# Weights and activations multiplied as plain float32, one product a tile, in place of three products of split float32r parts

## The chip, the cores and the metric

The kernel runs on one core of a Trainium2 chip. The metric is the device time of one launch in microseconds (us). Three runs of the kernel before gave 3092.03 us in the median (3088.94 to 3093.2).

## The reference

Two transformer stacks run one after the other on one sequence of 256 tokens by 1024 channels, all in float32. Cut to its products:

```python
# first stack, two layers: mixer, then FFN (layer 0 dense, layer 1 eight experts, top 2)
for layer in range(2):
    x = x + hybrid_mixer(rms_norm(x), w_in[layer], ...)   # 1024 x 9216, then three 1024 x 1024
    x = x + swiglu(h, w1, w3, w2)                         # layer 0: 1024 x 2816 twice, 2816 x 1024
    x = x + moe_swiglu(h, router_w, w1, w3, w2)           # layer 1: the same for each of 8 experts
x = rms_norm(x, final_norm)
# second stack, four layers: hyena, window attention, pooling, hyena; each with a swiglu
for i in range(4):
    x = x + mixer_i(rmsnorm(x))
    x = x + (silu(xn @ wg) * (xn @ wu)) @ wd
```

Nearly all arithmetic is activations times weights. The rest (chunked recurrence, convolutions by DFT, attention scores, routing, norms) works on tiles of the 256 tokens.

## The kernel before

Every weight matrix is cut into panels of 1 MB (128 partitions by 2048 floats; the last panel of each column block of an FFN's down projection has 1536). `panel_list` gives their order, and `sp_panels` (L236) loads them in that order from SyncE's queue into the `raw` ring of 6 places, each once panel i - 6 is `used`. A panel is 8 k-tiles of 256 columns in most products, so 16 weight tiles of 128x128, each met by the 256 tokens. For the experts it is 4 k-tiles of 512 columns (or 8 of 256), and in the expert's down projection 2 k-tiles of 1024; there the activations of 128 gathered tokens stand still in the array and the weights stream past.

TensorE gets float32r operands in two parts. ScalarE writes the rounded part of a panel into `whi`, a ring of 4 (`act_feed`, L251 to L260), and VectorE writes the rest, raw minus `whi`, over the raw panel as `wlo` (`dve_feed`, L263 to L271). `act_panel` and `dve_panel` put these instructions, up to three panels ahead, between the other work of the two engines; each engine works strictly in its order. Activations are kept in two parts as well: `act_high` or `act_ahead` on ScalarE, then `dve_low` (L470) or `dve_ahead` (L430) on VectorE. A tile's product is then three matmuls:

```python
e.matmul(o, wh, xh, start=first and t == k0, stop=False)   # L327
e.matmul(o, wh, xl, start=False, stop=False)               # L328
i = e.matmul(o, wl, xh, ...)                               # L329
```

L566 to L568, L1142 to L1144 (expert down), L1163 to L1165 (expert up and gate), L1997 to L1999 and L2233 to L2235 do the same for other shapes. `pe_panel` waits for both parts of the panel.

Other products were plain float32 before and stay so: the sums of squares (L354), the scores of the recurrence (L628), the DFTs (L1612, L1642, L1657), the scatter of expert outputs (L1212) and the transposes. The program text has one matmul for each such product.

Each stage is written by hand for each engine. In `pe_hgrn` the mixer's columns come in the order f, q, v, then ten half-steps with the recurrence's scores between them, gb, then `conv` on `CX`, `proj` on `OX`, `out` on `HX`. The last chunk of `CX` follows from `dve_conv` (L832), that of `HX` for `out` from L814, L816, `act_high` and L470. `pe_ffn` runs 11 pairs of panels and 12 down panels. `pe_moe` gathers tokens for a pair of experts (L1194), runs both experts and scatters (L1212).

Of the kernel before, what the change touches and what calls it, by code (L numbers as in the profile page):

```python
# [8 lines left out]
F32R = mybir.dt.float32r  # L9
# [7 lines left out]
L = 256  # L17
T8 = 8
# [4 lines left out]
NRAW = 6  # L23
NSPLIT = 4
# [14 lines left out]
def columns():  # L39
# [15 lines left out]
    "raw0", "raw1", "raw2", "raw3", "raw4", "raw5",  # L55
    "x_in", "ident_in", "vectors_in", "consts_in", "misc_in", "bias_in", "sink_in", "feat_in", "hy_in",
# [5 lines left out]
class Book:  # L62
# [6 lines left out]
    def restart(self, counting=False):  # L69
        self.counting = counting  # L70
        self.count = dict.fromkeys(self.sem, 0)
        self.turn, self.held, self.owner = 0, set(), [None] * 8
        self.panels = dict.fromkeys(("pe", "act", "dve"), 0)
        self.fed = dict.fromkeys(("act", "dve"), 0)
# [53 lines left out]
class Memory:  # L128
    def __init__(self, nc, ctx):
# [4 lines left out]
        self.HX = sb("HX", [128, 2, T8, L], F32R)  # L134
        self.HXP = nc.alloc_sbuf_tensor_at("HXP", [128, 2 * BUF], F32, offset=nc.sbuf_base - 8 * BUF)
        self.raw = sb("raw", [128, NRAW, BUF])
        self.wlo = nc.alloc_sbuf_tensor_at("wlo", [128, NRAW, BUF], F32R, offset=nc.sbuf_base - 4 * NRAW * BUF)
        self.whi = sb("whi", [128, NSPLIT, BUF], F32R)
# [11 lines left out]
        base = nc.sbuf_base - 4 * WORK  # L150

        def rounded(name, i, shape):
            return nc.alloc_sbuf_tensor_at(name, shape, F32R, offset=base + int(4 * BUF * i))

        self.OX = rounded("OX", 8, [128, 2, T8, L])
        self.CX = rounded("CX", 5, [128, 7, T8, L])[:, 0:7:6]
        self.HID = rounded("HID", 0, [128, 2, 22, L])
        self.HT = [rounded("HTH", 0, [128, 22, 128]), rounded("HTL", 1.5, [128, 22, 128])]
        self.GT = [rounded("GT0", 3, [128, 8, 2, L]), rounded("GT1", 5, [128, 8, 2, L])]
        self.SELR = rounded("SELR", 8, [128, 2, 2, 128])  # L160
        self.HXB = rounded("HXB", 6, [128, 2, T8, L])
# [23 lines left out]
def panel_list(a):  # L185
# [26 lines left out]
    hgrn(0)  # L212
    ffn(a["dense_w1"][0], a["dense_w3"][0], a["dense_w2"][0])
# [37 lines left out]
def act_feed(e, k, m, panels):  # L251
    i = k.fed["act"]
    if i == len(panels):
        return
    k.fed["act"] += 1
    n = width(panels[i])
    e.wait_ge(*k.at("raw", i))
    if i >= NSPLIT:
        e.wait_ge(*k.at("used", i - NSPLIT))
    e.activation(m.whi[:, i % NSPLIT, 0:n], m.raw[:, i % NRAW, 0:n], ACT.Copy).then_inc(*k.up("act", "hi", i))  # L260


def dve_feed(e, k, m, panels):  # L263
    i = k.fed["dve"]
    if i == len(panels):
        return
    k.fed["dve"] += 1
    n = width(panels[i])
    e.wait_ge(*k.at("hi", i))
    hi = m.whi[:, i % NSPLIT, 0:n].bitcast(F32)  # L270
    e.tensor_tensor(m.wlo[:, i % NRAW, 0:n], m.raw[:, i % NRAW, 0:n], hi, ALU.subtract).then_inc(*k.up("dve", "lo", i))  # L271


def act_panel(e, k, m, panels):

    k.panels["act"] += 1
    while k.fed["act"] < min(k.panels["act"] + NSPLIT - 1, 2 * k.panels["act"] + 1, len(panels)):
        act_feed(e, k, m, panels)


def dve_panel(e, k, m, panels):
    k.panels["dve"] += 1
    while k.fed["dve"] < min(k.panels["dve"] + NSPLIT - 1, 2 * k.panels["dve"] + 1, len(panels)):
        dve_feed(e, k, m, panels)


def pe_panel(e, k, m):
    i = k.panels["pe"]
    k.panels["pe"] += 1
    e.wait_ge(*k.at("hi", i))  # L290
    e.wait_ge(*k.at("lo", i))
    return i


def weights(m, i, kt, n):
    both = m.whi[:, i % NSPLIT, 0:kt * n], m.wlo[:, i % NRAW, 0:kt * n]
    return [w.rearrange("p (k n) -> p k n", k=kt) for w in both]
# [21 lines left out]
def pe_weights_still(e, k, o, w, c, x, k0, k1, kx, first=True, final=True, fresh=None):  # L319

    i = None
    for t in range(k0, k1):
        wh, wl = (v[:, t, c:c + 128] for v in w)
        xh, xl = x[:, 0, kx + t, :], x[:, 1, kx + t, :]
        if fresh:
            e.wait_ge(*k.at(*fresh, kx + t))
        e.matmul(o, wh, xh, start=first and t == k0, stop=False)  # L327
        e.matmul(o, wh, xl, start=False, stop=False)  # L328
        i = e.matmul(o, wl, xh, start=False, stop=final and t == k1 - 1)  # L329
    return i  # L330


def pe_gemm(e, k, m, s, name, x, cols, fresh=None, after=None):

    for j in cols:
        i = pe_panel(e, k, m)
        w = weights(m, i, 8, 256)
        o = pe_take(e, k, m, "g", s, name, j)
        pe_weights_still(e, k, o[:, 0:L], w, 0, x, 0, 8, 0, fresh=fresh)
        fresh = None  # L340
        pe_weights_still(e, k, o[:, L:2 * L], w, 128, x, 0, 8, 0).then_inc(*k.up("mm", "g", s, name, j))
# [37 lines left out]
def act_norm(e, k, m, s, h, rstd):  # L379
    act_rstd(e, k, m, s, rstd)  # L380
    for c in range(T8):
        e.wait_ge(*k.at("h", s, c))
        e.activation(m.HX[:, 0, c, :], h[:, c, :], ACT.Copy).then_inc(*k.up("act", "hh", s, c))


def dve_scale(e, k, m, s, c, h, rstd, gain):
# [11 lines left out]
def dve_norm(e, k, m, s, h, rstd, gain):  # L398
    for c in range(T8 + 1):
        if c < T8:  # L400
            dve_scale(e, k, m, s, c, h, rstd, gain)
# [2216 lines left out]
```

## Time and profile before

| | |
|---|---|
| median of 3 runs | 3092.03 us |
| the profiled execution, device time | 3087.74 us |
| its span in the profile | 3085.9 us |
| TensorE matmul busy | 2980.6 us (97%) |
| VectorE busy | 2039.1 us (66%) |
| ScalarE busy | 1632.0 us (53%) |
| granted TensorE clock, mean | 0.98 of full |
| read from HBM | 608.99 MB |

Busy time of TensorE counts pipelined matmuls once. The duration of one record (0.28 us for one of 256 columns) is its latency, longer than the distance to the next record's start. What a stream of matmuls costs is read from the starts. The chain of waits lists each step with that distance.

### The profile page before, as it was taken

What the parts mean: (1) busy time and instruction counts of PE and PEld (TensorE: products, weight loads), DVE (VectorE), ACT (ScalarE), POOL (GpSimd) and SP (SyncE); (2) the same over time, 40 slices, a digit from 0 to 9 for tenths busy, and PEclk for the clock granted to TensorE, in tenths of its full rate; (3) what the DMA queues carried; (4) which work ended last, traced back from release to release, by engine and by line L of the source; (5) the groups of instructions that cost most, each with busy time, mean ns of one, the idle gap of its engine ahead of it and who ended that gap; (6) DMA issues with size and microseconds to landing.
All of it is one profiled execution on the core that took longest, in us unless ns stands there. A gap on an engine that the chain in (4) does not pass through costs nothing.

```text
span 3085.9 us, 46925 instructions
## 1 busy us (share of the span) xinstructions
PE 2980.6 (97%) x20370; PEld 2732.1 (89%) x20370; DVE 2039.1 (66%) x1833; ACT 1632.0 (53%) x1593; POOL 260.0 (8%) x199
## 2 busy tenths in 40 slices
PE   7999999999979999999999899999899999999999
PEld 7998999999878888888788596999799999886999
DVE  5786665578648888888789665554555455565553
ACT  5446444544537767777677452444654444363442
POOL 1130110013000000000000102010001001012010
PEclk9999999999979999999999899999999999999999
DMA  6444555544428989989989240556255555431453
GB/s 206 156 139 144 157 178 177 179 151 144 144 98 347 356 341 375 350 339 358 367 341 371 93 137 28 166 183 213 82 160 178 195 164 172 157 107 58 137 179 122
DMA packets 358818, 613.14 MB, mean 199 GB/s; under 512 B 11375, under 2 KB 323397, under 8 KB 323536
## 3 DMA queue, kind: packets, MB, share of 16 engines
q1 hardware_dynamic: 354592, 597.73, 55.5%
q10 hardware_dynamic: 3536, 12.23, 1.2%
q8 instruction: 164, 2.69, 0.4%
q14 instruction: 46, 0.38, 0.0%
q0 software_dynamic: 480, 0.12, 0.0%
HBM read 608.99 MB, written 1.05 MB: 198 GB/s over the span
## 4 chain that ended last, share of the span: by engine, by line
PE 86%; DVE 5%; ACT 5%; issue 2%; DMA 1%; ACTq 0%; DVEq 0%
PE ps L327 16%; PE ps L328 16%; PE ps L329 16%; PE ps L1163 5%; PE ps L1165 5%; PE ps L1164 5%; PE ps L1144 3%; PE ps L1142 3%; PE ps L1143 2%; PE ps L1642 2%; PE ps L628 2%; PE ps L1657 2%; ACT whi L260 2%; PE ps L1612 1%; DVE wlo L271 1%
## 5 line engine op out<-in xcount | busy, mean ns | idle before, releaser
L271 DVE TENSOR_TENSOR wlo<-raw,whi 128x2048 fp32r<-128x2048 f32 (+1 forms) x573 | 1315.4, 2301 | 633.6 <-ACT whi L260 629.5
L260 ACT ACTIVATE whi<-raw 128x2048 fp32r<-128x2048 f32 (+1 forms) x573 | 1083.7, 1894 | 271.1 <-PE ps L329 139.6
L327 PE MATMUL ps<-HX,whi 128*128 128x256 f32 x1808 | 520.5, 288 | 26.2 <-DVE HX L470 10.7
L328 PE MATMUL ps<-HX,whi 128*128 128x256 f32 x1808 | 514.8, 285 | 0.0
L329 PE MATMUL ps<-HX,wlo 128*128 128x256 f32 x1808 | 514.8, 285 | 0.0
L327 PE MATMUL ps<-HXB,whi 128*128 128x256 f32 x1760 | 500.3, 284 | 0.0
L329 PE MATMUL ps<-HXB,wlo 128*128 128x256 f32 x1760 | 498.1, 283 | 0.0
L328 PE MATMUL ps<-HXB,whi 128*128 128x256 f32 x1760 | 498.0, 283 | 0.0
L327 PEld LDWEIGHTS ps<-HX,whi 128*128 128x128 f32 x1808 | 350.4, 194 | 29.6 <-DVE HX L470 16.3
L328 PEld LDWEIGHTS ps<-HX,whi 128*128 128x128 f32 x1808 | 350.4, 194 | 0.6 <-issue 0.2
L329 PEld LDWEIGHTS ps<-HX,wlo 128*128 128x128 f32 x1808 | 350.2, 194 | 0.0
L327 PEld LDWEIGHTS ps<-HXB,whi 128*128 128x128 f32 x1760 | 337.9, 192 | 0.7 <-issue 0.3
L328 PEld LDWEIGHTS ps<-HXB,whi 128*128 128x128 f32 x1760 | 337.8, 192 | 0.3
L329 PEld LDWEIGHTS ps<-HXB,wlo 128*128 128x128 f32 x1760 | 337.8, 192 | 0.0
L1163 PE MATMUL ps<-whi,GT 128*128 128x512 f32 (+1 forms) x768 | 289.4, 377 | 4.7 <-DVE wlo L271 4.3
L1165 PE MATMUL ps<-whi,GT 128*128 128x512 f32 (+1 forms) x768 | 286.3, 373 | 0.0
L1164 PE MATMUL ps<-wlo,GT 128*128 128x512 f32 (+1 forms) x768 | 285.8, 372 | 0.0
L327 PE MATMUL ps<-HID,whi 128*128 128x256 f32 x880 | 251.2, 285 | 0.0
L329 PE MATMUL ps<-HID,wlo 128*128 128x256 f32 x880 | 249.1, 283 | 0.0
L328 PE MATMUL ps<-HID,whi 128*128 128x256 f32 x880 | 249.0, 283 | 0.0
L1163 PEld LDWEIGHTS ps<-whi,GT 128*128 128x128 f32 x768 | 145.1, 189 | 29.9 <-DVE wlo L271 3.8
L327 PEld LDWEIGHTS ps<-HID,whi 128*128 128x128 f32 x880 | 168.9, 192 | 0.3
(318 smaller groups left out, 4382.6 us busy)
## 6 DMA issues: line engine op xcount, KB each, us to landing
raw<-in_c_experts SPq DMA_DIRECT2D x264, 1024.0 KB, 4.9
raw<-in_w_in SPq DMA_DIRECT2D x72, 1024.0 KB, 5.0
raw<-in_ff_w_gate SPq DMA_DIRECT2D x44, 1024.0 KB, 5.3
raw<-in_ff_w_up SPq DMA_DIRECT2D x44, 1024.0 KB, 5.3
raw<-in_ff_w_down SPq DMA_DIRECT2D x32, 1024.0 KB, 5.1
raw<-in_dense_w SPq DMA_DIRECT2D x30, 1024.0 KB, 5.3
raw<-in_hy_w_in SPq DMA_DIRECT2D x24, 1024.0 KB, 5.2
raw<-in_ff_w_down SPq DMA_DIRECT2D x16, 768.0 KB, 4.5
```

What stands on the lines that cost most here:

```text
L260: e.activation(m.whi[:, i % NSPLIT, 0:n], m.raw[:, i % NRAW, 0:n], ACT.Copy).then_inc(*k.up("act", "hi", i))
L271: e.tensor_tensor(m.wlo[:, i % NRAW, 0:n], m.raw[:, i % NRAW, 0:n], hi, ALU.subtract).then_inc(*k.up("dve", "lo", i))
L327: e.matmul(o, wh, xh, start=first and t == k0, stop=False)
L328: e.matmul(o, wh, xl, start=False, stop=False)
L329: i = e.matmul(o, wl, xh, start=False, stop=final and t == k1 - 1)
L628: mm = e.matmul(o[:, c * 128:(c + 1) * 128], lhs[:, hh], rhs[:, hh], start=True, stop=True)
L1142: e.matmul(o[c][:, :], hh, wh[:, kk, cs], start=t == 0, stop=False)
L1143: e.matmul(o[c][:, :], hh, wl[:, kk, cs], start=False, stop=False)
L1144: mm = e.matmul(o[c][:, :], hl, wh[:, kk, cs], start=False, stop=t == 21)
L1163: e.matmul(o[:, 0:n], xh, wh[:, t, :], start=first, stop=False)
L1164: e.matmul(o[:, 0:n], xh, wl[:, t, :], start=False, stop=False)
L1165: mm = e.matmul(o[:, 0:n], xl, wh[:, t, :], start=False, stop=last)
```

## The change

The split goes. Panels are multiplied from the place where they land, in float32, with activations kept once, in float32. The `raw` ring has 10 places, in the room of `whi` and the second half of the activations. Both engines' feeds go (L251 to L284), as do all high and low parts. The gather of the experts' tokens makes one float32 product where it made two float32r ones. Smaller edits come with it:

- the first panel of the program comes in two halves, x as well, and the six DMAs of constants that ScalarE issued are issued by SyncE behind the first ten panels; the sums of squares of x come after the first gemm in place of before it (`pe_first`)
- activations for the next gemm are scaled by ScalarE for even chunks and by VectorE for odd ones (`act_ahead`, `dve_ahead`)
- the first tap of the mixer's convolution is a ScalarE instruction (`taps`), and chunks 4 to 7 are convolved before the norm of gb in place of behind it
- the four norms of o come together behind the first conv panel, and the output leaves in four DMAs

```diff
-NRAW = 6
-NSPLIT = 4
+NRAW = 10
-def act_feed(e, k, m, panels):
-    e.activation(m.whi[:, i % NSPLIT, 0:n], m.raw[:, i % NRAW, 0:n], ACT.Copy).then_inc(*k.up("act", "hi", i))
-def dve_feed(e, k, m, panels):
-    e.tensor_tensor(m.wlo[:, i % NRAW, 0:n], m.raw[:, i % NRAW, 0:n], hi, ALU.subtract).then_inc(*k.up("dve", "lo", i))
+def pe_panel(e, k, m, kt, n):
+    i = k.panels
+    k.panels += 1
     e.wait_ge(*k.at("raw", i))
+    return i, m.raw[:, i % NRAW, 0:kt * n].rearrange("p (k n) -> p k n", k=kt)
...
-        e.matmul(o, wh, xh, start=first and t == k0, stop=False)
-        e.matmul(o, wh, xl, start=False, stop=False)
-        i = e.matmul(o, wl, xh, start=False, stop=final and t == k1 - 1)
+        i = e.matmul(o, w[:, t, c:c + 128], x[:, kx + t, :], start=first and t == k0, stop=final and t == k1 - 1)
...
+def pe_first(e, k, m, s, last):
+    for h in range(2):
+        i, w = pe_panel(e, k, m, 4, 256)
+        halves.append(w)
+        pe_weights(e, k, o[:, 0:L], w, 0, m.HX, 0, 4, 4 * h, first=h == 0, final=h == 1, fresh=("hx", last))
+    for h in range(2):
+        mm = pe_weights(e, k, o[:, L:2 * L], halves[h], 128, m.HX, 0, 4, 4 * h, first=h == 0, final=h == 1)
...
-                    e.matmul(o[c][:, :], hh, wh[:, kk, cs], start=t == 0, stop=False)
-                    e.matmul(o[c][:, :], hh, wl[:, kk, cs], start=False, stop=False)
-                    mm = e.matmul(o[c][:, :], hl, wh[:, kk, cs], start=False, stop=t == 21)
+                    mm = e.matmul(o[c][:, :], m.HT[:, t, :], w[:, kk, c * 512:c * 512 + 512], start=t == 0, stop=t == 21)
...
+    def taps(cs):
+        e.wait_ge(*k.at("free", "g", s, "u", 3))
+        for c in cs:
+            e.activation(m.buf8(5)[:, c, :], conv_rows(m)[:, c, 0:L], ACT.Copy, scale=m.col("conv_w", 24 * l + c)).then_inc(
+                *k.up("act", "tap", s, c))
...
     for j in range(4):
-        dve_panel(e, k, m, panels)
+        dve_conv(e, k, m, s, l, (4 + j,))
         dve_times_norm(e, k, m, s, last, "gb", j, m.buf(1)[:, j * 512:j * 512 + 512])
-        dve_conv(e, k, m, s, l, (4 + j,))
...
-    e.dma_start(out, m.X[:, :, :]).then_inc(*k.land("out_done", "out"))
+    for c0, c1 in ((0, 4), (4, 6), (6, 7), (7, 8)):
+        for c in range(c0, c1):
+            e.wait_ge(*k.at("x", last, c))
+        e.dma_start(out[:, c0:c1, :], m.X[:, c0:c1, :]).then_inc(*k.land("out_done", "out"))
```

TensorE's queue from the start of the program before (`HX` is the activations, `ones` serves the sums of squares):

```order
L354 MATMUL ps<-work,ones 128x256 x6
L327 MATMUL ps<-HX,whi 128x256
L328 MATMUL ps<-HX,whi 128x256
L329 MATMUL ps<-HX,wlo 128x256
L327 MATMUL ps<-HX,whi 128x256
```

The same queue now (`rows` is the activations, `raw` the panels as landed):

```order
L275 MATMUL ps<-rows,raw 128x256 x16
L307 MATMUL ps<-work,ones 128x256 x8
L275 MATMUL ps<-rows,raw 128x256 x112
L381 MATMUL ps<-ident,rs 128x128 x2
L283 MATMUL ps<-raw,rows 128x256 x64
```

The 48 matmuls of a panel are 16, and the sums of squares stand behind the first of them.

VectorE's queue before, from the last chunk of the mixer's convolution through the conv products to the start of `proj`'s:

```order
L842 SCALAR_TENSOR_TENSOR work<-work,par 128x256
L845 TENSOR_TENSOR work<-work 128x256
L470 TENSOR_TENSOR CX<-work,CX 128x256
L271 TENSOR_TENSOR wlo<-raw,whi 128x2048
L808 TENSOR_TENSOR work<-work,ps 128x512
L796 SCALAR_TENSOR_TENSOR work<-work,par 128x512
L800 TENSOR_TENSOR work<-work 128x512
L796 SCALAR_TENSOR_TENSOR work<-work,par 128x512
L800 TENSOR_TENSOR work<-work 128x512
L470 TENSOR_TENSOR OX<-work,OX 128x256 x4
L271 TENSOR_TENSOR wlo<-raw,whi 128x2048
```

And now (L366 is the norm of the last gb panel):

```order
L755 SCALAR_TENSOR_TENSOR work<-work,par 128x256
L757 SCALAR_TENSOR_TENSOR work<-work,par 128x256
L760 TENSOR_TENSOR work<-work 128x256
L366 TENSOR_TENSOR work<-ps,rs 128x512
L729 TENSOR_TENSOR work<-work,ps 128x512
L719 SCALAR_TENSOR_TENSOR work<-work,par 128x512
L723 TENSOR_TENSOR work<-work 128x512
L719 SCALAR_TENSOR_TENSOR work<-work,par 128x512
L723 TENSOR_TENSOR work<-work 128x512
```

The last chunk of the convolution is complete before the last gb panel is normed, and neither a low part nor a panel's split stands between.

## Rows read from the trace of the kernel before

**Rows 1.** The page: busy time by engine; granted TensorE clock in 40 slices.

```profile
PE 2980.6 (97%) x20370; PEld 2732.1 (89%) x20370; DVE 2039.1 (66%) x1833; ACT 1632.0 (53%) x1593; POOL 260.0 (8%) x199
...
PEclk9999999999979999999999899999999999999999
```

**Rows 2.** The page: costliest groups, the two feeds.

```profile
L271 DVE TENSOR_TENSOR wlo<-raw,whi 128x2048 fp32r<-128x2048 f32 (+1 forms) x573 | 1315.4, 2301 | 633.6 <-ACT whi L260 629.5
L260 ACT ACTIVATE whi<-raw 128x2048 fp32r<-128x2048 f32 (+1 forms) x573 | 1083.7, 1894 | 271.1 <-PE ps L329 139.6
```

**Rows 3.** Chain of waits, last FFN: start us, us to the next, what.

```profile
3068.12 0.12 PE ps L327
...
3071.72 0.12 PE ps L327
```

**Rows 4.** Chain of waits, an expert's down projection.

```profile
999.93 0.23 PE ps L1144
...
1001.97 0.23 PE ps L1144
```

**Rows 5.** Timeline of PE, plain float32 streams: start us, us, what, records.

```profile
1138.57 7.07 PE L1212 MATMUL ps<-work 128*128 128x256 f32 x32
...
1877.90 13.98 PE L1657 MATMUL ps<-work 128*128 128x256 f32 x64
...
1759.57 8.32 PE L1612 MATMUL ps<-work 128*128 128x512 f32 x19
```

**Rows 6.** PE groups by line and shape: xcount | busy us, mean ns | idle before.

```profile
L327 PE MATMUL ps<-HX,whi 128*128 128x256 f32 x1808 | 520.5, 288 | 26.2 <-DVE HX L470 10.7 <-DVE wlo L271 6.3 <-issue 4.9
...
L327 PE MATMUL ps<-HXB,whi 128*128 128x256 f32 x1760 | 500.3, 284 | 0.0
...
L1163 PE MATMUL ps<-whi,GT 128*128 128x512 f32 x640 | 252.6, 395 | 4.7 <-DVE wlo L271 4.3 <-ACT GT L1280 0.3
L327 PE MATMUL ps<-HID,whi 128*128 128x256 f32 x880 | 251.2, 285 | 0.0
...
L1142 PE MATMUL ps<-whi,HTH 128*128 128x512 f32 x352 | 138.5, 394 | 0.0
...
L327 PE MATMUL ps<-CX,whi 128*128 128x256 f32 x128 | 39.7, 310 | 11.8 <-DVE CX L470 11.8
```

**Rows 7.** Whom PE waited for: us in total, times, longest us.

```profile
PE ps L327 <- DVE CX L470: 11.8, 2, 5.9
...
PE ps L327 <- DVE HX L470: 10.7, 3, 5.2
...
PE ps L1938 <- ACT small L2067: 5.2, 2, 2.7
PE ps L327 <- issue: 4.9, 2, 3.6
...
PE ps L1163 <- DVE wlo L271: 4.3, 2, 3.4
PE ps L327 <- ACT HX L466: 4.2, 2, 2.1
```

**Rows 8.** Timeline of the start, PE.

```profile
9.46 4.53 PE L354 MATMUL ps<-work,ones 128*128 128x256 f32 x12 [9.46 <-ACT work L361]
20.33 0.55 PE L327 MATMUL ps<-HX,whi 128*128 128x256 f32 x1 [6.34 <-DVE wlo L271]
```

**Rows 9.** Windows behind three waits, PE: us, PE busy (records), PEclk, DMA share, GB/s.

```profile
275.70:282.60 6.90, 2.97 (x14) 0.51 0.00 1
...
866.20:873.10 6.90, 5.67 (x26) 0.51 0.00 0
1531.80:1535.30 3.50, 3.50 (x10) 0.51 1.02 424
```

**Rows 10.** Window over the experts: us, PE, PEld, DVE, ACT, POOL, PEclk, DMA, GB/s.

```profile
926.20:1717.60 791.40, 785.05 (x3772) 660.12 (x3772) 671.05 (x399) 572.12 (x405) 0.00 (x0) 1.00 0.92 353
```

**Rows 11.** Timeline of the end, the output's DMA, in a span of 3085.9.

```profile
3081.63 0.36 SPq L2336 DMA_DIRECT2D out<-X  x1
```

## What the change will do: the prediction

> **What bounds the kernel now.** I read the page's busy times first: TensorE is busy for 2980.6 of 3085.9 us, VectorE for two thirds and ScalarE for half [rows 1]. The two feeds look expensive, 1315.4 us of VectorE and 1083.7 us of ScalarE [rows 2], but both engines wait for TensorE or for each other most of the time, so they count only where TensorE waits for them. I therefore read next whom TensorE waited for [rows 7], and last how far apart its matmuls start, from the chain of waits [rows 3, 4] and the timeline [rows 5]. The reader is to see that TensorE is idle for 3085.9 - 2980.6 = 105 us in all, and that the change's sign depends on one comparison: three float32r matmuls against one plain float32 product.
>
> **A tile of 256 columns before.** From 3068.12 to 3071.72 the chain has 30 steps [rows 3], 3.60 / 30 = 0.120 us each, so three make 0.360 us.
>
> **A tile of 512 columns before.** From 999.93 to 1001.97 there are 9 steps [rows 4], 0.227 us each, so three make 0.680 us.
>
> **A plain float32 product.** The text has 16 matmuls for one scatter (4 x 2 x 2 in `pe_scatter`), yet the timeline has 32 records for it [rows 5]; the start shows 12 records for 6 matmuls of L354 [rows 8]. Every plain product is thus two records, and each record takes long. L1657 has 64 records of 256 columns in 13.98 us; less the latency of the last one (0.38), that is 13.60 / 63 = 0.216 us each. L1212 gives the same: (7.07 - 0.38) / 31 = 0.216. One product of 256 columns is 0.432 us. L1612 has 19 records of 512 columns in 8.32 us: (8.32 - 0.59) / 18 = 0.429, so a product is 0.859 us. The weights change with every product in L1657 and L1612, both operands come from SBUF, and the clock is full, as it will be here. float32r pays its 0.120 with a change of weights each time as well.
>
> So a tile of 256 columns gets slower by 0.432 - 0.360 = 0.072 us, one of 512 by 0.859 - 0.680 = 0.179 us.
>
> A page of the Trainium skill bears on this. "FP8 and Floating Point Precision", TensorE Precision Notes, says that true FP32 takes four passes through the array; "TensorE: Matmul & The Clock Gate", Back-to-back issue gap, gives a warm pass N / 2.4 + 2.5 ns. Four such passes are 0.437 and 0.863 us, an estimate from the pages. The rows say 0.432 and 0.859, so here two of the four passes share one record and its fixed cost. The same formula gives a float32r pass of 256 columns 0.109 us, and the row's 0.120 disagrees; the row decides. By the pages' cost of the new products alone the sum below would be 28 us higher.
>
> **How many tiles.** The first of the three matmuls is counted by shape [rows 6]: 1808 (HX) + 1760 (HXB) + 880 (HID) + 128 (CX), three more groups of 128 that the text gives (OX, the experts' last columns, the v columns) and two of 16 (attention's v, pooling) make 4992 of 256 columns; 640 + 352 = 992 have 512. 4992 x 0.072 = 359 us, and 992 x 0.179 = 178 us. The gather of a pair of experts goes from 32 float32r matmuls (3.84 us) to 16 plain ones (6.9 us), four times: 12 us. Together +549 us. The text's other products stay.
>
> **What comes back.**
> - The start. The first gemm begins at 20.33 us, 6.34 us after the early sums and waiting for `wlo` [rows 8]. Now half of x, half a panel and one scaling suffice. I take 8 to 9 us, since ScalarE's first work on x ended before the sums began at 9.46. Of these 12 us, 2.6 go to the six sums that used to run in the idle time, and about 1.3 to more tiles at the half clock. Gain 8 us.
> - The waits of the mixers. CX 11.8, HX 10.7, two "issue" waits 4.9 (one of them behind VectorE's scan, where a split stood queued), the experts' `wlo` 4.3, the hyena's HX 4.2 [rows 7]: 35.9 us. In each the last chunk now needs one or two instructions where it needed four, and `out` has six tiles of 0.43 us to run before it wants that chunk. What is late next is the last evacuation of `proj`, two VectorE instructions of 512 columns, which I estimate from the duration of a 2048-column one [rows 2] at under 2 us with their waits, against 2.6. I take all 35.9.
> - Attention's waits for ScalarE, 5.2 [rows 7], where feeds stood between squares. I take 5.
> - The clock. Behind each of these waits the granted clock fell from 1.0 to 0.5, 1.2 GHz of 2.4: at 275.7, 866.2 and 1531.8 [rows 9], and three times more. A stretch holds 14 to 26 matmuls of 0.213 us in place of 0.120 (about 2 us), the expert's 10 lose 0.2 each. Six together 11 us.
> - The end. The output's DMA starts at 3081.63 and ends the span at 3085.9 [rows 11], 4.3 us for 1 MB. The last of four pieces is an eighth: 2 us less.
>
> That is 8 + 36 + 5 + 11 + 2 = 62 us. VectorE loses 1315 us and ScalarE 1084 us of feeds and gain nothing by it otherwise; the taps, copies and scalings that move to ScalarE are below 1 us each and lie beside gemms. The ring of ten panels gains nothing either: over the experts the DMA engines moved 353 GB/s [rows 10] in 791 us; now the same bytes have some 980 us, 285 GB/s. The waits that I leave (routing, the branch before the second stack, hyena's transposes, some 45 us) depend on chains that the change barely shortens.
>
> **The sum.** The profiled execution took 3087.7 us: 3087.7 + 549 - 62 = 3575. It lies 4.3 us below the median of the three runs, so the time forecast for the median is 3579 us, 16% slower. The bounds: none of the waits behind the start returned gives 3087.7 + 549 - 10 + 4 = 3631; all of TensorE's idle time and some 25 us of half clock returned gives 3087.7 + 549 - 130 + 4 = 3511.
>
> **The rivals.**
> 1. Much more comes back (3511 us). For it: VectorE and ScalarE are half empty afterwards, and every handover has fewer steps. Against: routing and the second stack's start wait for chains without a feed in them. 8%.
> 2. Little comes back (3631 us). The waits named move to what is late next, the POOL's norms or ScalarE's longer chain at `on`, and the half clock with them. For it: all four `on` products now stand behind the first conv panel and read squares that ScalarE makes from the o products. Against: a panel now takes 6.9 us where it took 5.8, so each such chain has more cover. 13%.
> 3. The new products cost the pages' four full passes, or weights that come from a place beside a landing DMA cost a little more: 3607 us. 6%.
> 4. Faster: each new product is one record of 0.216 (0.429) us. The mechanism would be that the second record belongs to something particular to the old plain products. Then the tiles change by 4992 x -0.144 + 992 x -0.251 = -968 us, less 62; the experts would be bound by DMA, 264 panels or 277 MB at the 353 GB/s of [rows 10] being 785 us against 511 us of matmuls, which gives 274 back: about 2330 us. The change is a gain as soon as a 256-column product costs under about 0.37 us. Against it: three lines of different operands all show two records per product. 2%.
> 5. The clock stays at 0.5 in these streams, over 6000 us. L1612 and L1657 ran at the full clock through tens of us. 1%.
>
> **How the numbers follow.** My forecast, between about 3545 and 3615, has 70%. With part of rivals 1 to 3 the range of 3535 to 3622 holds the time 8 times in 10. A change under 0.2% (6 us) couldn't be told from none. Faster 2% (rival 4), the same 1%, slower 97%.
>
> **What would show it.** In the changed profile the L275 matmuls have two records for each in the text (about 9,984 of 256 columns), with starts 0.216 us apart; expert records are 0.429 apart; TensorE is over 97% busy; the first gemm begins at 8 to 9 us; no wait stands before the conv or out gemm of either mixer; the slices over the experts move some 285 GB/s. I am wrong if records of 256 columns start less than 0.18 us apart or come one to a product, if the idle time of TensorE exceeds 80 us, or if the clock falls in the middle of a gemm.

## The result, and the profile after

The changed kernel took 3563.56 us in the median of 4 runs (3561.89 to 3567.58), the kernel before 3092.61 us in the runs beside it: a ratio of 1.1527, with a 95% interval of 1.1508 to 1.1547, so it is 15% slower. The forecast was 3579 us, 15 us more. Profile against profile the execution took 3562.73 us where before took 3087.74: +475.0 us, and the forecast was +487.

The page of the changed kernel, busy times and clock, answers to [rows 1]:

```profile
PE 3506.4 (98%) x14386; PEld 2643.8 (74%) x14386; DVE 625.7 (18%) x1019; ACT 502.4 (14%) x850; POOL 213.5 (6%) x199
...
PEclk9999999999989999999999899999999999999999
```

TensorE has 14386 records in place of 20370 and is busy 526 us longer. VectorE lost 1413 us and ScalarE 1130 us, and nothing was won by it. The groups of matmuls by line and shape of the changed kernel (count, busy time, latency of one, idle time before) answer to [rows 6]:

```profile
L275 PE MATMUL ps<-work,raw 128*128 128x256 f32 x5792 | 1254.9, 379 | 0.0
L275 PE MATMUL ps<-rows,raw 128*128 128x256 f32 x3616 | 790.5, 380 | 8.9 <-DMA raw<-in_w_in 8.9
L1052 PE MATMUL ps<-raw,work 128*128 128x512 f32 x1280 | 554.7, 592 | 0.3 <-ACT work L1163 0.3
L1035 PE MATMUL ps<-raw,work 128*128 128x512 f32 x704 | 304.8, 592 | 0.0
L283 PE MATMUL ps<-raw,rows 128*128 128x256 f32 x320 | 69.7, 379 | 0.0
...
L1052 PE MATMUL ps<-raw,work 128*128 128x256 f32 x256 | 56.6, 379 | 0.0
```

5792 + 3616 + 320 + 256 = 9984 records of 256 columns are two for each of 4992 tiles, and 1280 + 704 = 1984 are two for each of 992. The pace stands in the changed kernel's chain of waits (start, us to the next, what, records), which answers to [rows 3, 4]:

```profile
252.37 41.44 PE ps L275 x192
...
2263.12 170.94 PE ps L275 x792
```

170.94 / 792 = 0.216 us for a record of 256 columns. In an expert's up and gate products (L1052) 10 records of 512 columns take 4.29 us, 0.429 each:

```profile
1179.96 4.29 PE ps L1052 x10
```

Whom TensorE waited for in the changed kernel (us in total, times, longest) answers to [rows 7]:

```profile
PE ps L275 <- DMA raw<-in_w_in: 8.9, 1, 8.9
PE ps L1460 <- issue: 5.8, 1, 5.8
PE ps L1493 <- DVE work L1701: 5.4, 2, 2.7
PE ps L992 <- DVE work L335: 3.9, 1, 3.9
PE ps L1004 <- DVE work L1206: 3.7, 1, 3.7
PE ps L1780 <- ACT small L1900: 3.1, 2, 1.5
```

No wait for the activations of `conv` or `out` is left. What is left are the first panel's landing, the second stack's beginning (L1460), the hyenas, the routing (L992, L1004) and attention. All of TensorE's idle time is 3560.9 - 3506.4 = 54.5 us, where it was 105.3. The changed kernel's timeline of the start and of the end answers to [rows 8, 11]:

```profile
8.88 9.15 PE L275 MATMUL ps<-rows,raw 128*128 128x256 f32 x32 [8.88 <-DMA raw<-in_w_in]
17.87 3.62 PE L307 MATMUL ps<-work,ones 128*128 128x256 f32 x16
...
3555.99 2.92 SPq L2140 DMA_DIRECT2D out<-X  x2
3558.13 0.42 DVE L886 TENSOR_TENSOR X<-X,ps 128x256 f32<-128x256 f32 x1 [2.17 <-PE ps L275]
```

The first gemm starts at 8.88 us, 11.5 us sooner. The span ends at 3560.9, 2.4 us after VectorE's last addition; before, it ended 4.4 us after that addition. A window over the experts of the changed kernel (us, PE, PEld, DVE, ACT, POOL, granted clock, DMA share, GB/s) answers to [rows 10]:

```profile
1030.00:2005.00 975.00, 973.82 (x2644) 484.42 (x2643) 46.23 (x86) 72.50 (x129) 0.00 (x0) 1.00 0.81 287
```

The DMA engines moved 287 GB/s in place of 353, with a share of 0.81 in place of 0.92, and TensorE was busy for 973.8 of the 975 us.

### The profile page after: what moved, and what is told of

The parts are those of the page before. It is cut to its first block, busy times and chain, and to the rows that moved or that the text cites. A ratio compares the mean times of both kernels' runs of the same rounds, so it can differ in the third digit from the quotient of the medians.

```text
span 3560.9 us, 32658 instructions
## 1 busy us (share of the span) xinstructions
PE 3506.4 (98%) x14386; PEld 2643.8 (74%) x14386; DVE 625.7 (18%) x1019; ACT 502.4 (14%) x850; POOL 213.5 (6%) x199
## 4 chain that ended last, share of the span: by engine, by line
PE 97%; ACT 1%; DVE 1%; issue 0%; POOL 0%; DMA 0%; ACTq 0%; SPq 0%; POOLq 0%; DVEq 0%
PE ps L275 57%; PE ps L1052 17%; PE ps L1035 8%; PE ps L283 2%; PE ps L1504 2%; PE ps L568 2%; PE ps L1519 2%; PE ps L1474 1%; PE ps L307 1%; PE ps L1083 1%; PE ps L1460 1%; PE ps L1101 1%; PE ps L1069 1%; PE ps L1814 0%; PE ps L2056 0%
## 5 line engine op out<-in xcount | busy, mean ns | idle before, releaser
L275 PE MATMUL ps<-work,raw 128*128 128x256 f32 x5792 | 1254.9, 379 | 0.0
L275 PEld LDWEIGHTS ps<-work,raw 128*128 128x128 f32 x5792 | 1100.2, 190 | 150.7 <-issue 1.3
L275 PE MATMUL ps<-rows,raw 128*128 128x256 f32 x3616 | 790.5, 380 | 8.9 <-DMA raw<-in_w_in 8.9
L275 PEld LDWEIGHTS ps<-rows,raw 128*128 128x128 f32 x3616 | 686.6, 190 | 102.8 <-DMA raw<-in_w_in 8.9
L1052 PE MATMUL ps<-raw,work 128*128 128x512 f32 (+1 forms) x1536 | 611.3, 557 | 0.3 <-ACT work L1163 0.3
L1052 PEld LDWEIGHTS ps<-raw,work 128*128 128x128 f32 x1536 | 289.5, 190 | 301.0 <-issue 294.2
L1035 PE MATMUL ps<-raw,work 128*128 128x512 f32 x704 | 304.8, 592 | 0.0
L1035 PEld LDWEIGHTS ps<-raw,work 128*128 128x128 f32 x704 | 132.5, 190 | 160.7 <-issue 160.7
L366 DVE TENSOR_TENSOR work<-ps,rs 128x512 f32<-128x512 f32 x84 | 58.0, 691 | 775.5 <-issue 526.5
L864 POOL TENSOR_TENSOR work<-work,rs 128x512 f32<-128x512 f32 x55 | 69.7, 1268 | 1092.1 <-ACT work L853 1092.1
L372 POOL TENSOR_TENSOR work<-work,rs 128x512 f32<-128x512 f32 x40 | 51.2, 1280 | 371.4 <-ACT work L575 370.7
L283 PE MATMUL ps<-raw,rows 128*128 128x256 f32 x320 | 69.7, 379 | 0.0
L1474 PE MATMUL ps<-work 128*128 128x512 f32 x128 | 60.6, 635 | 3.1 <-issue 3.1
L1504 PE MATMUL ps<-work 128*128 128x512 f32 x128 | 58.2, 612 | 3.1 <-ACT work L1569 3.0
```

The lines of the kernel that those rows point to most:

```text
L275: i = e.matmul(o, w[:, t, c:c + 128], x[:, kx + t, :], start=first and t == k0, stop=final and t == k1 - 1)
L283: i = e.matmul(o[:, j * 256:j * 256 + 256], x[:, t, j * 128:j * 128 + 128], w[:, t, :], start=t == t0, stop=t == t1 - 1)
L366: e.tensor_tensor(dst.rearrange("p (a n) -> p a n", a=2), o, m.wide_rs, ALU.mult).then_inc(*k.up("dve", "free", "g", s, name, j))
L372: e.tensor_tensor(v, v, m.wide_rs, ALU.mult).then_inc(*k.up("pool", *event))
L864: e.tensor_tensor(v, v, m.wide_rs, ALU.mult).then_inc(*k.up("pool", "sil normed", s, j))
L1035: mm = e.matmul(o[c][:, :], m.HT[:, t, :], w[:, kk, c * 512:c * 512 + 512], start=t == 0, stop=t == 21)
```

## Where the 475 us come from

From the matmul records of both traces I worked out an account of the span: for each pair of neighbours, the distance of their starts less the median distance of that line and shape at the full clock. What is over 0.4 us counts as a wait; what is less counts as half clock where the granted clock was 0.5.

| | before | after | difference | forecast |
|---|---|---|---|---|
| records at their full-clock pace | 2924.5 | 3472.1 | +547.6 | +549 |
| waits between records | 111.6 | 59.9 | -51.7 | -49 |
| half clock | 26.5 | 10.5 | -16.0 | -11 |
| the rest of short gaps | 8.7 | 6.3 | -2.4 | 0 |
| before the first and behind the last record | | | about -2.5 | -2 |

The sum is +475. (These waits begin at the median distance and not at the end of a record's latency, so they add up to more than the page's idle time.) The new products cost what the rows of the old plain ones said. The waits came back nearly as forecast in size. This doesn't say which part of the change gave them back. The experiments are about that.

## Experiments on the changed kernel

Each expectation says what its own theory A and theory B are. In the first, theory A is the prediction's: the handovers to TensorE have fewer steps, so their waits go. Theory B: the steps don't matter; a panel now takes 6.9 us of TensorE in place of 5.8, and this covers the same chains.

**plain_in_old.** The kernel before, feeds, low parts and waits all kept, with one plain matmul a tile (here at L327; the five other sites alike). The low parts enter no product, so this kernel leaves them out of its result:

```diff
-        e.matmul(o, wh, xh, start=first and t == k0, stop=False)
-        e.matmul(o, wh, xl, start=False, stop=False)
-        i = e.matmul(o, wl, xh, start=False, stop=final and t == k1 - 1)
+        i = e.matmul(o, wh.bitcast(F32), xh.bitcast(F32), start=first and t == k0, stop=final and t == k1 - 1)
```

> The kernel before with one thing changed: each weight tile is met by one plain float32 product of the two high parts, in place of three float32r products. Both engines still make every high and low part, and TensorE still waits for both; the low parts enter no product, so that part of the result is left out. Theory A (the price of the product makes the slowdown, and the rest of the change gave back some 75 us): 4992 x 0.072 + 992 x 0.175 = 533 us on top of 3092, less what the longer gemms hide by themselves, so 3600 to 3625 us. Theory B (the feeds' removal gives back nothing, the longer gemms hide the old waits by themselves): within 10 us of the changed kernel less its 12 us of dearer gathers, so 3545 to 3560 us.

3569.45 us, ratio 1.1546 (1.1527 to 1.1565). Both ranges missed it, and B was nearer, by 9 us against 31. The time is 6 us above the changed kernel's, 18 if one adds the 12 us by which its gathers are cheaper. What is left of waits behind a feed or a handover of `HX`:

```profile
PE ps L327 <- DVE wlo L271: 5.4, 1, 5.4
...
PE ps L327 <- ACT HX L464: 4.2, 2, 2.1
```

The 11.8 us for CX and the 10.7 us for HX [rows 7] are gone although no step of the handovers was taken away. So a longer panel is enough to remove them, and the prediction's reason isn't needed for it. The account of the span, worked out for this run as well, says where it differs from the changed kernel: about 12 us less for the gathers, and against that 12 us more of waits, 4 of half clock and 3 before the first and behind the last record.

**ring6, old_start, old_mixer_order.** In each of these, one group of the smaller edits of the changed kernel is undone: `NRAW = 6` in place of 10; the first panel whole and the sums of squares before the first gemm; the taps on VectorE, conv behind gb's norm and the norms of o in two pairs.

```diff
-NRAW = 10
+NRAW = 6
```

```diff
-    for c0 in (0, 4):
-        e.dma_start(m.X[:, c0:c0 + 4, :], a["c_x"][:, c0:c0 + 4, :]).then_inc(*k.land(f"x{c0 // 4}_in"))
...
+    e.dma_start(m.X[:, :, :], a["c_x"]).then_inc(*k.land("x0_in"))
```

```diff
-        w1, w2 = (m.col("conv_w", (l * 3 + j) * 8 + c) for j in (1, 2))
-        e.wait_ge(*k.at("tap", s, c))
+        w0, w1, w2 = (m.col("conv_w", (l * 3 + j) * 8 + c) for j in range(3))
...
+        e.tensor_scalar(o, vp[:, c, 0:L], w0, None, ALU.mult).then_inc(*k.up("dve"))
```

> The changed kernel with 6 panel places in place of 10. Theory A (DMA is late nowhere): no change, 3560 to 3570 us. Rival (the deeper ring is what removed the two waits over the experts, 4.3 us and the half clock behind them): 3568 to 3575 us, with waits of PE for DMA of raw.

> The changed kernel with the start of before: x and the first panel whole, the constants' DMAs on ScalarE's queue ahead of its work, the sums of six chunks before the first gemm. Theory A: the first gemm begins some 4 to 5 us later (at 13 to 14 us in place of 8.9), but 2.6 us of sums move into the idle time, so 1 to 3 us slower. Rival (the start edits carry the whole gain of 8 us at the start): 3571 us.

> The changed kernel with the mixer's old order in both layers: the first tap on VectorE, chunks 4 to 7 convolved behind the norm of gb, the norms of o in two pairs. Theory A (the waits of 11.8 us for CX went because the split's instructions went): no wait comes back, 3560 to 3567 us. Rival (they went by the new order): 10 to 18 us slower, 3574 to 3582 us, with PE waiting for VectorE's last chunk before the conv gemm.

They took 3564.32, 3563.09 and 3562.75 us against 3563.56: undone one at a time, none of the three moves the time beyond its spread from run to run. With old_start the first gemm began at 14.06 us in place of 8.88, but by then twelve records of the sums of squares were done, and its 32 records took 7.07 us, 0.216 each. In the changed kernel the 32 took 9.15 us: its first ten start about 0.43 us apart, twice the distance of the rest, and those slow records are here among the sums of squares, of which the first ten cost as much. The rows of old_start:

```profile
14.06 7.07 PE L273 MATMUL ps<-rows,raw 128*128 128x256 f32 x32
20.96 1.03 PE L305 MATMUL ps<-work,ones 128*128 128x256 f32 x4
```

The same 48 records are done by 21.83 us here and by 21.32 in the changed kernel.

## The loop that TensorE waited for

A longer panel can only cover a wait if what TensorE waits for has a period of its own. The kernel before's timeline of VectorE over the gb panels of the first mixer, its feeds only:

```profile
253.20 2.29 DVE L271 TENSOR_TENSOR wlo<-raw,whi 128x2048 fp32r<-128x2048 f32 x1 [1.38 <-ACT whi L260]
...
260.14 2.29 DVE L271 TENSOR_TENSOR wlo<-raw,whi 128x2048 fp32r<-128x2048 f32 x1 [1.38 <-ACT whi L260]
...
267.08 2.29 DVE L271 TENSOR_TENSOR wlo<-raw,whi 128x2048 fp32r<-128x2048 f32 x1 [1.37 <-ACT whi L260]
```

and of ScalarE in the same place:

```profile
258.21 1.90 ACT L260 ACTIVATE whi<-raw 128x2048 fp32r<-128x2048 f32 x1
263.06 0.63 ACT L646 ACTIVATE work<-work 128x512 f32<-128x512 f32 x1 [2.96 <-DVE work L439]
264.82 0.42 ACT L466 ACTIVATE CX<-work 128x256 fp32r<-128x256 f32 x1 [1.13 <-DVE work L845]
265.15 1.90 ACT L260 ACTIVATE whi<-raw 128x2048 fp32r<-128x2048 f32 x1
```

Each engine waits for the other, in a ring: ScalarE's feed (1.90), VectorE's feed of the same panel (2.29), the norm and the convolution (about 2.4 with their steps), the start of ScalarE's high part of CX, and 0.33 us behind that start ScalarE's next feed. The period is 6.94 us. TensorE needs 48 x 0.120 = 5.8 us for a panel, so it runs 1.2 us away from the loop with each panel, until `conv` finds the last chunk of CX 5.9 us late [rows 7]. With plain products a panel takes 32 x 0.216 = 6.91 us, nearly the loop's own period, and no debt builds up. plain_in_old shows this: its loop has the same 6.94 us (VectorE's timeline), and `conv` doesn't wait.

```profile
289.00 2.29 DVE L271 TENSOR_TENSOR wlo<-raw,whi 128x2048 fp32r<-128x2048 f32 x1 [1.37 <-ACT whi L260]
...
295.94 2.29 DVE L271 TENSOR_TENSOR wlo<-raw,whi 128x2048 fp32r<-128x2048 f32 x1 [1.37 <-ACT whi L260]
```

Neither engine is busy all the time in this loop, which is why their busy shares of 66% and 53% didn't show it. From here on theory A is this loop, and theory B the prediction's number of steps. The timelines are those of the gb panels; for HX and `proj` the loop is inferred from what the experiments do to that wait.

**one_rounded.** The kernel before with the first of each three matmuls alone (the five other sites alike). The products with low parts are left out, so its result is coarser:

```diff
-        e.matmul(o, wh, xh, start=first and t == k0, stop=False)
-        e.matmul(o, wh, xl, start=False, stop=False)
-        i = e.matmul(o, wl, xh, start=False, stop=final and t == k1 - 1)
+        i = e.matmul(o, wh, xh, start=first and t == k0, stop=final and t == k1 - 1)
```

> The kernel before with one float32r product per tile, that of the two high parts; the low parts are made as before but leave the products, so the result is coarser than the reference. By the rows of before, tiles then cost 4992 x 0.120 + 992 x 0.227 = 824 us in place of 2472, and TensorE alone would end at about 1440 us. Theory A (the loop of ScalarE's feed, VectorE's feed, norm and scaling has a period of 6.94 us for a gb panel whatever TensorE does, and TensorE waits by as much as its panel is shorter): gb panels come every 6.9 us with about 1.9 us of matmuls in each, the waits for HX, CX and the feeds grow from 36 us to hundreds, and the time is 1900 to 2400 us. Theory B (the waits belong to the number of steps at a handover, which is unchanged here): the waits stay near 100 us and the time is 1440 to 1600 us, or what the DMA engines need for the weights.

2755.09 us in one run, 355 above theory A's range and 1155 above theory B's. TensorE has 1174 us less of busy time, but the time fell by 337 us only, and TensorE is idle for 946 us. The timeline of VectorE in one_rounded over the gb panels:

```profile
238.91 2.29 DVE L271 TENSOR_TENSOR wlo<-raw,whi 128x2048 fp32r<-128x2048 f32 x1 [1.38 <-ACT whi L260]
...
245.84 2.29 DVE L271 TENSOR_TENSOR wlo<-raw,whi 128x2048 fp32r<-128x2048 f32 x1 [1.38 <-ACT whi L260]
...
252.78 2.29 DVE L271 TENSOR_TENSOR wlo<-raw,whi 128x2048 fp32r<-128x2048 f32 x1 [1.38 <-ACT whi L260]
```

The period is 6.93 us again, with 16 matmuls (1.9 us at the full clock) to a panel in place of 48. The loop doesn't depend on TensorE's pace. The longest rows of waits ("issue" is a wait to which the profile can put no releaser):

```profile
PE ps L327 <- issue: 285.7, 113, 12.4
PE ps L1157 <- DVE wlo L271: 123.3, 106, 4.7
```

**half_feeds.** The kernel before, with as many matmuls and steps, each feed from the seventh panel on half as wide (ScalarE's and VectorE's alike). The other half of a panel is not split, and a product that wanted its low part reads the place of its high part, so the result is incomplete:

```diff
+    n = n if i < NRAW else n // 2
...
+        wl = wl if 2 * t < w[0].shape[1] else wh
```

> The kernel before with each feed from the seventh panel on cut to half the panel (ScalarE 1.90 to about 0.95 us, VectorE 2.29 to about 1.15); the other half is left unsplit, and its products read what stands in the high buffer, so the result is incomplete. Number, order and duration of the matmuls and every wait are unchanged. Theory A (the loop of the feeds, 6.94 us a gb panel against TensorE's 5.77, is what TensorE waits for): the loop falls to about 4.9 us, TensorE sets the pace, and the waits for CX and HX (22.5 us), one behind the scan and the experts' wlo 4.3 go, with some of the half clock: 3045 to 3062 us. Theory B (the waits belong to the number of steps that follow the last matmul): those steps are the same, and 3080 us or more remain.

3044.65 us, ratio 0.9848 (0.9833 to 0.9864), just under the range of theory A. Nothing about the number of steps changed, and 47 us came back. The waits for CX are gone, and of those for HX behind VectorE 0.5 us is left. By itself this run can't tell the loop from the two engines' plain load, which fell too; dve_behind below can.

**split_reordered.** The kernel before, split kept, with the order of its instructions changed: in the mixers the last feed of a row of panels stands behind what hands over to TensorE, the conv chunks stand before gb's norm, the first panel's feed stands before the squares, the output leaves in four DMAs. Its core on VectorE:

```diff
     for j in range(4):
-        dve_panel(e, k, m, panels)
+        if j < 3:
+            dve_panel(e, k, m, panels)
+        dve_conv(e, k, m, s, l, (4 + j,))
         dve_times_norm(e, k, m, s, last, "gb", j, m.buf(1)[:, j * 512:j * 512 + 512])
-        dve_conv(e, k, m, s, l, (4 + j,))
+    dve_panel(e, k, m, panels)
```

> The kernel before, split kept, with only its order changed: the feeds of the mixers' panels stand behind the operations that hand over to TensorE, the first panel's feed and HX stand before the squares, the early sums after the first panel, and the output leaves in four DMAs. Theory A (waits come from the feeds' loop standing in the chain that hands over): of the 36 us of mixer waits, 12 to 25 go, the start gives 3 to 6, the end 1 to 2: 3050 to 3070 us. If the loop's period of 6.94 us per panel against TensorE's 5.77 is all that counts, wherever a feed stands, the waits move to the panels instead and 3080 to 3095 us remain. Theory B (number of steps at a handover): the steps there are the same, so only the start and the end move: 3080 to 3088 us.

3074.93 us, ratio 0.9944 (0.9931 to 0.9958), above theory A's range and below both theory B's and that of the remark on the loop, so the reorder bought less than A said. TensorE still waits 7.7 us of 11.8 for CX and 5.7 of 10.7 for HX, which fits a feed that is moved within the loop and stays in it.

**dve_behind.** The kernel before with VectorE's feed two panels ahead in place of three, ScalarE's still three:

```diff
-    while k.fed["dve"] < min(k.panels["dve"] + NSPLIT - 1, 2 * k.panels["dve"] + 1, len(panels)):
+    while k.fed["dve"] < min(k.panels["dve"] + NSPLIT - 2, 2 * k.panels["dve"] + 1, len(panels)):
```

> The kernel before with one constant changed: VectorE's feed runs two panels ahead instead of three, ScalarE's still three. Nothing else moves. In the gb panels VectorE's feed then finds its high part ready and needn't wait 1.38 us for ScalarE, so that by theory A the loop falls from 6.94 to about 5.5 us, under TensorE's 5.77: the wait for CX at the end of those panels goes in both mixers and part of HX: 3070 to 3083 us, unless a panel elsewhere comes late by it, above all in the experts, where wlo was waited for already (4.3 us). By theory B nothing changes: 3088 to 3095 us.

3070.05 us, ratio 0.9929 (0.9915 to 0.9942), at the lower edge of theory A's range. Its timeline of VectorE over the gb panels:

```profile
255.27 2.28 DVE L271 TENSOR_TENSOR wlo<-raw,whi 128x2048 fp32r<-128x2048 f32 x1
...
260.74 2.28 DVE L271 TENSOR_TENSOR wlo<-raw,whi 128x2048 fp32r<-128x2048 f32 x1
...
266.21 2.28 DVE L271 TENSOR_TENSOR wlo<-raw,whi 128x2048 fp32r<-128x2048 f32 x1
```

The wait of 1.38 us for ScalarE is gone, the period is 5.47 us, below TensorE's 5.8, and the wait for CX with it; of the 10.7 us for HX 0.5 is left. Matmuls, feeds and steps are all as before, so neither less work nor fewer steps were needed, only the same work one panel later. It has a price elsewhere: the experts' matmuls of L1163 wait 6.2 us for `wlo` where it was 4.3, and L327 waits 10.2 us for `wlo` and 8.8 for "issue" where it was 6.3 and 4.9.

**reordered_behind.** split_reordered with this constant too; its diff is the one above.

> split_reordered (3074.9 us, split kept) with VectorE's feed two panels ahead instead of three. If the feeds' loop is what is left in its CX and HX waits (13.4 us and the half clock behind them), 3055 to 3070 us; if the two edits buy the same waits, 3070 to 3078 us.

3053.24 us, ratio 0.9879 (0.9864 to 0.9894): 2 us below its range. The two edits gave 17.5 and 22.0 us alone and 38.8 together, so they buy different waits. It keeps the split and its three products, and is faster than both kernels of this case, than the one before by 1.2%. What it waits for:

```profile
PE ps L327 <- DVE wlo L271: 15.5, 1, 15.5
PE ps L1619 <- ACT work L361: 5.9, 1, 5.9
PE ps L1652 <- DVE work L1873: 5.4, 2, 2.7
PE ps L327 <- issue: 5.2, 2, 2.7
PE ps L1959 <- ACT small L2088: 5.0, 2, 3.2
```

CX has no wait left and HX behind VectorE has 0.5 us. The longest row is the start. Of waits for a feed behind it, the experts keep 4.8 us for `wlo`, the longest 3.8. The half clock fell with the waits, from 124 us in 18 stretches of the span to 85 us in 11.

**one_fed.** One float32r product of high parts a tile, and no low part of the weights:

```diff
 def dve_feed(e, k, m, panels):
...
     k.fed["dve"] += 1
...
-    hi = m.whi[:, i % NSPLIT, 0:n].bitcast(F32)
-    e.tensor_tensor(m.wlo[:, i % NRAW, 0:n], m.raw[:, i % NRAW, 0:n], hi, ALU.subtract).then_inc(*k.up("dve", "lo", i))
...
-    e.wait_ge(*k.at("lo", i))
```

> One float32r product per tile from the high parts, and VectorE's feed taken away altogether, so no low parts of weights exist; the result is coarser than the reference. TensorE's matmuls are those of one_rounded (2755 us). By theory A the loop of a gb panel falls from 6.94 to about 4.6 us and VectorE loses 1304 us, so the time falls by several hundred us, to 2000 to 2350 us; ScalarE's 573 copies (1077 us) beside its other work (540 us) and the DMA engines (609 MB at the 353 to 410 GB/s seen over the experts, 1500 to 1730 us) are next. If instead TensorE's slower clock between waits (0.76 on average in one_rounded) sets the time, less than 200 us goes.

2196.58 us, ratio 0.7105 (0.7092 to 0.7118): 559 us below one_rounded with the same matmuls. That is what VectorE's feed held up there, by the loop and by its 1304 us of work together. What is left of the loop is ScalarE's copies: TensorE waits for `whi` for 298 us in three lines. The result is coarser than both kernels', so this is no substitute where the low parts are wanted. Its page shows what is next, the DMA engines over the experts (busy tenths, and GB/s):

```profile
DMA  9756999747479999999999970708972998927099
GB/s 303 225 180 204 289 326 322 235 154 230 157 313 422 404 410 421 399 409 422 411 397 421 422 262 0 230 1 279 349 266 82 345 329 253 348 90 230 1 317 296
```

## What a record of each kind costs

Two kernels stream 128 of the 256 columns in all matmuls of a 256-column group but the first, one on the changed kernel and one on the kernel before. Half of their result's columns are incomplete, and each ran once. The edit on the changed kernel:

```diff
-        i = e.matmul(o, w[:, t, c:c + 128], x[:, kx + t, :], start=first and t == k0, stop=final and t == k1 - 1)
+        n = 256 if first and t == k0 else 128
+        i = e.matmul(o[:, 0:n], w[:, t, c:c + 128], x[:, kx + t, 0:n], start=first and t == k0, stop=final and t == k1 - 1)
```

**cols128_plain.**

> The changed kernel, where in the gemms of 256 columns all matmuls of a group but its first stream 128 columns, so half of the result's columns are incomplete. If the plain product costs by its columns, the two records of a product lie about 0.110 us apart each, and the time falls by 4992 products x 7/8 (those that shrink) x 2 x 0.106 = about 920 us less what waits come in its place, to 2650 to 2850 us. If loading float32 weights for each of the two records is a floor, they stay above 0.15 us.

2701.86 us. The median distance of starts is 0.112 us for its 8371 records of 128 columns at the full clock, beside 0.216 at 256 and 0.429 at 512. From 256 to 512 columns the time doubles to within 3 ns, so there a plain record pays for its columns, and two records of 0.216 were the right price of 256 columns.

**cols128_split.**

> The kernel before, where in the gemms of 256 columns all matmuls of a group but its first stream 128 columns, so half of the result's columns are incomplete. This measures the float32r record by itself. If it costs by its columns, starts lie about 0.060 to 0.067 us apart; if the 0.120 us at 256 columns is held up by a fixed cost of loading weights (the 0.227 at 512 columns less 0.120 leaves 0.013 beyond the columns), they lie 0.067 us apart; if the weight load is a floor of its own, they stay at 0.110 to 0.120 us (records of 128 columns elsewhere in this kernel started 0.112 apart), and the feeds' loop bounds the kernel meanwhile, so starts inside a panel are read, not the time.

3158.08 us, 66 us more than before with half of the columns. The chain of waits in it, inside a panel:

```profile
599.95 0.11 PE ps L328
600.07 0.11 PE ps L329
```

The median is 0.111 us, where 256 columns took 0.120 and 512 took 0.227. From 512 to 256 columns a record loses 0.107 us and from 256 to 128 only 0.009, as the third guess had it: a float32r matmul with new weights has a floor of about 0.11 us. The kernel before shows that the floor isn't float32r's alone. It has plain float32 records with 1 column (L1618), 64 (L1972) and 128 (L628), with a weight load each, and the median distance of their starts at the full clock is 0.112 us for all three. Its timeline of two such streams:

```profile
108.64 3.74 PE L628 MATMUL ps<-work 128*128 128x128 f32 x32
...
2725.54 1.84 PE L1618 MATMUL ps<-ones,work 128*128 128x1 f32 x16
```

So 0.112 for a plain record of 128 columns is that floor too, and only at 256 and more does the plain record pay for its columns. That the floor is the loading of weights is my reading; no run here separates it.

The reason why the time rose is the clock. The window over 130 us of a mixer in cols128_split (us, PE busy and records, PEld, DVE, ACT, POOL, granted clock, DMA share, GB/s):

```profile
2745.60:2875.20 129.60, 127.75 (x585) 124.95 (x585) 49.71 (x60) 49.00 (x72) 0.00 (x0) 0.50 0.31 98
```

TensorE is busy for 127.8 of 129.6 us and its clock is 0.5 (1.2 GHz) all the while; 585 records at 0.213 us are 124.6 us. Over the whole span the clock was 0.5 for 493 us in 23 stretches, against 124 us in 18 in the kernel before, with the same number of records in the same order. At 0.5 a record of 128 columns takes the 0.213 us that one of 256 columns takes too. By the account of the section above, half clock cost some 164 us more than before, where the shorter records saved 98. cols128_plain, with records as short (0.112), spent only 75 us in 9 stretches at 0.5. Which property of the stream brought the clock down is open, and cols128_split ran only once.

## Why the prediction was right, and where it was not

- **The price of a product** (+359, +178, +12): right. The account gives +547.6 where the terms had +549. The chain's 0.216 and 0.429 are the rows' numbers to the nanosecond, with two records a product. Rival 4 fell with the count of 9984 and 1984 records. Rival 3 found nothing to stand on: the median record paid no more with panels landing beside it. By the Trainium skill, four passes ("FP8 and Floating Point Precision", TensorE Precision Notes) at the warm pace that "TensorE: Matmul & The Clock Gate", Back-to-back issue gap, gives for an isolated matmul would be 0.437 and 0.863 us, an estimate; the traces show 0.432 and 0.858 in the median.
- **The waits of the mixers, the experts and the hyena** (36 us): the size was right, the reason wrong. The failed step is "In each the last chunk now needs one or two instructions where it needed four". plain_in_old keeps all four and has no CX or HX wait behind VectorE; half_feeds and dve_behind keep them too, at the old price of a product, and lose the CX wait and all but 0.5 us of the HX wait. What was late was the loop of 6.94 us a panel, not the last chunk's steps. Rival 2 held the cover as its own counterargument ("a panel now takes 6.9 us where it took 5.8, so each such chain has more cover"), and plain_in_old shows that it is enough by itself. But the changed kernel has both, longer panels and no feeds, and half_feeds shows that shorter feeds alone are enough as well. No run parts the two, so that the 36 us came out right is luck as far as the reason goes. The same holds for the experts' `wlo` (4.3 us, 0.5 in plain_in_old).
- **The hyena's and the first gemm's waits** are the part that the longer panel doesn't give: ScalarE's HX 4.2 us and `wlo` at the start 5.4 us stand in plain_in_old and not after.
- **The start** (8 us): the first gemm began at 8.88 us as said, but old_start shows that the rearranged start earned nothing. The gain is that of a start without a split.
- **Attention** (5 us): 2.1 came back, and 3.1 stayed.
- **The half clock** (11 us): 16.0 came back, and 2.4 of short gaps. I had counted the stretches behind six waits. The clock was at 0.5 for 124 us before and 72 after (7 recorded stretches, none of them within a gemm of L275), and some of those that vanished stood behind waits which the prediction hadn't listed, such as at 1862.9 and 2200.9.
- **The end** (2 us): right, 2.0 us from VectorE's last addition to the end.
- **Nothing for the feeds' time and for the ring**: right. VectorE and ScalarE lost 2543 us between them and the time rose; ring6 moved nothing. Over the experts the DMA engines moved 287 GB/s, where 285 were expected.

The 12 us between the forecast and the result, profile to profile, are 5 of half clock, 3 of waits, 2 of short gaps and 2 of everything else.

What stays open: whether the longer panel or the missing feeds would have to be credited in the changed kernel, where each is enough, and what lowers the clock in a busy stream of float32r.

## What to carry to other kernels

Price a new product from a stream of the same type and the same number of columns in the same trace, record by record, and count the records against the text. Where an engine waits once at the end of a row of panels, look for a loop among the other engines whose period is longer than a panel: their busy shares don't show it, the even distance of one instruction's starts does, and letting one side run a step behind can break it without removing any work. A wait that goes when the waiting engine gets slower has not been repaired, only covered.

## What was not expected of the hardware

- A record with new weights has a floor near 0.11 us in both types. float32r takes 0.111 at 128 columns, 0.120 at 256, 0.227 at 512; a plain float32 record takes 0.112 at 1, 64 and 128 columns, 0.216 at 256 and 0.429 at 512, and a product has two of them. Three float32r matmuls beat one plain product at 256 and 512 columns (0.360 to 0.432, 0.681 to 0.858), and at 128 columns they would lose (0.333 to 0.224, an estimate from these figures).
- Halving the columns of the float32r stream made the kernel 2% slower in its one run, since the granted clock was 0.5 for 493 us of a span in which TensorE was 96% busy.
